# Two attention heads side by side on TensorE, values by channel, and the block export ahead of the slabs

## The reference, cut to what matters

```
q = rms_norm(q) * 64**-0.5 ; k = rms_norm(k)
p = softmax over keys of (q k^T + bias by distance, by three dilated windows)
out = p v
```

## Time and profile before

| | |
|---|---|
| median of 3 runs | 1527.39 us |
| lowest, highest | 1512.98, 1580.74 us |
| the profiled execution | 1512.7 us, span 1510.8 us |
| PE busy | 1414.2 us (94%) |
| DVE, ACT, POOL busy | 504.5, 253.1, 175.2 us |
| mean granted clock | 0.94 |

### The profile page before, as it was taken

One profiled execution on the slowest core, in us unless ns is written; L12 is line 12 of the kernel. 1 busy time (PEld: TensorE's weight loads), 2 busy tenths in 40 slices (PEclk: granted clock), 3 DMA queues, 4 the chain that ended last, 5 costly groups with the idle time before them and its releaser, 6 DMA issues.

```text
span 1510.8 us, 15332 instructions
## 1 busy us (share of the span) xinstructions
PE 1414.2 (94%) x5616; PEld 757.4 (50%) x5616; DVE 504.5 (33%) x1149; ACT 253.1 (17%) x491; POOL 175.2 (12%) x168
## 2 busy tenths in 40 slices
PE   5999989999969999999999859999999999999985
PEld 3444655544437777777455534344444444444432
DVE  2089673233523545555134530211111111111110
ACT  5000223232012323333011100000000000000000
POOL 1000015221000000000000010211110111111111
PEclk9999999999956878899999859999999999999998
DMA  6011010100020101030322139886999999999971
GB/s 258 0 57 56 0 56 1 57 6 22 0 93 5 32 5 32 4 116 1 115 88 94 56 116 424 318 339 243 405 420 403 400 412 397 402 396 398 402 288 22
DMA packets 51273, 262.17 MB, mean 174 GB/s; under 512 B 21571, under 2 KB 21843, under 8 KB 38908
## 3 DMA queue, kind: packets, MB, share of 16 engines
q1 hardware_dynamic: 42684, 244.18, 40.2%
q0 software_dynamic: 8320, 16.81, 4.6%
q10 hardware_dynamic: 192, 0.17, 0.0%
HBM read 247.97 MB, written 23.64 MB: 180 GB/s over the span
## 4 chain that ended last, share of the span: by engine, by line
PE 72%; issue 9%; DMA 6%; DVE 6%; POOL 3%; DVEq 2%; ACT 1%; SPq 0%; POOLq 0%; ACTq 0%
PE ps L1137 19%; PE ps L1139 13%; PE ps L869 9%; PE ps L1046 7%; PE ps L1001 6%; PE ps L1024 4%; PE ps L1013 3%; DMA arena<-in_ex_up 3%; DMA arena<-in_ex_down 2%; POOL arena L1971 2%; PE ps L1123 1%; PE ps L1067 1%; POOL arena L1967 1%; DVEq L1249 1%; DVE arena L1250 1%
## 5 line engine op out<-in xcount | busy, mean ns | idle before, releaser
L1137 PE MATMUL ps<-arena 128*128 128x512 f32 x768 | 338.0, 597 | 1.7 <-ACT arena L1922 0.8
L1137 PEld LDWEIGHTS ps<-arena 128*128 128x128 f32 x768 | 144.7, 192 | 172.5 <-issue 170.1
L1139 PE MATMUL ps<-arena 128*64 128x512 f32 x480 | 212.1, 598 | 7.6 <-DMA arena<-in_ex_up 4.1
L1140 PE MATMUL ps<-arena 128*64 128x512 f32 x480 | 212.2, 598 | 0.0
L873 PE MATMUL ps<-arena 128*128 128x512 f32 x384 | 172.0, 601 | 0.0
L869 PE MATMUL ps<-arena 128*128 128x512 f32 x320 | 137.6, 592 | 0.0
L1139 PEld LDWEIGHTS ps<-arena 128*64 128x64 f32 x480 | 64.4, 138 | 136.5 <-issue 134.5
L1693 DVE TENSOR_TENSOR arena<-arena,ps 128x512 f32<-128x512 f32 x26 | 17.9, 689 | 330.1 <-PE ps L1137 204.1
L873 PEld LDWEIGHTS ps<-arena 128*128 128x128 f32 x384 | 72.5, 194 | 81.7 <-issue 81.6
L1046 PE MATMUL ps<-arena 128*128 128x512 f32 x256 | 111.0, 592 | 0.0
L1001 PE MATMUL ps<-arena 64*128 64x512 f32 (+3 forms) x192 | 96.5, 617 | 14.6 <-DVE arena L1456 13.6
(11 more groups left out here) (296 smaller groups left out, 1298.2 us busy)
## 6 DMA issues: line engine op xcount, KB each, us to landing
arena<-in_ex_gate SPq DMA_DIRECT2D x32, 2048.0 KB, 21.5
arena<-in_ex_up SPq DMA_DIRECT2D x32, 2048.0 KB, 24.3
arena<-in_ex_down SPq DMA_DIRECT2D x32, 2048.0 KB, 24.0
arena<-in_w_in SPq DMA_DIRECT2D x5, 2048.0 KB, 8.0
arena<-in_x SPq DMA_DIRECT2D x16, 512.0 KB, 6.4
arena<-bias_by_distance SPq DMA_DIRECT2D x4, 1024.0 KB, 5.8
arena<-in_w_out SPq DMA_DIRECT2D x8, 512.0 KB, 7.5
out<-arena SPq DMA_DIRECT2D x8, 512.0 KB, 2.7
```

The lines of the kernel that those rows point to most:

```text
L1137: last = mm(ps[:, to, :], rowsT[:, k, :], weights[left][:, k, cols], **f)
L1139: mm(ps[0:HALF, to, :], rowsT[:, k, 0:HALF], weights[left][:, k, cols], **f)
L1140: last = mm(ps[HALF:P, to, :], rowsT[:, k, HALF:P], weights[right][:, k, cols], **f)
```

## The change

Attention steps become 32 double steps: both heads of a pair for one tile. Tiles run from 7 to 0 in pairs 0 and 2, and from 0 to 7 in pairs 1 and 3. Scores are cut in chunks of at most 512 keys; one chunk fills bank 6 with one head and bank 7 with the other, and the reductions run on each head and chunk, with the maxima of two chunks joined after. Values take v as the weight (64 columns) and `probT` as the moving side, head 0 to partitions 0 to 63 of bank 3 and head 1 to 64 to 127, so the result is already channels by tokens. The old turns of `att` (`att_out`) go; instead the reciprocals of the sums are spread over 64 columns each (`rz`), turned (`zt`), copied by ACT to `rzb`, and multiplied onto bank 3 by DVE (`att`). Values of step m-1 stand before the turns of step m, and `probT` has one buffer. The DeltaNet pieces go to two slots of a double step. The first double step's scores stand among the last v tiles. On SP the export of the inverse goes before all but slab 0, slab 0 waits for the k projections alone, and the order constants are loaded at the stage's end. Pool clears the pads in two parts. Seven blocks of constants that nothing reads (`C_LVL`, 896 columns) are dropped, and some buffers move (`slab`, `prob`, `T`, `mixT_dn`, `hg`, `h2s`, `xs`, two of `w_out`, `actT`).

```diff
+STEP_PAIRS = AT_HEADS // 2
+N_STEPS = STEP_PAIRS * TILES
+
+
+def attention_step(m):
+
+    pair, k = divmod(m, TILES)
+    return pair, (k if pair % 2 else TILES - 1 - k)
+
+
+def score_chunks(m):
+
+    wide = (attention_step(m)[1] + 1) * P
+    return [(c0, min(512, wide - c0)) for c0 in range(0, wide, 512)]
+
+
+CHUNKS = [(m, c) for m in range(N_STEPS) for c in range(len(score_chunks(m)))]
+CHUNKS_PER_PAIR = len(CHUNKS) // STEP_PAIRS
...
     attention = []
-    for n in range(n_att + 8):
-        if n < n_att:
-            attention.append((("scores", n), 1.5 * attention_step(n)[1] + 2))
-        if 1 <= n <= n_att:
-            attention.append((("turn", n - 1), 1.5 * attention_step(n - 1)[1] + 2))
-        if 2 <= n <= n_att + 1:
-            attention.append((("values", n - 2), 0.5 * attention_step(n - 2)[1] + 1))
-        if n % 8 == 4 and n >= 12:
-            attention.append((("att_out", n // 8 - 1), 1))
+    for m in range(N_STEPS + 1):
+        if m + 1 < N_STEPS:
+            attention.append((("scores", m + 1, 0), 0.45))
+        if m:
+            attention.append((("values", m - 1), 0.3 * (attention_step(m - 1)[1] + 1) + 0.5))
+            if m % 4 == 0:
+                attention.append((("att", m // 4 - 1), 0))
+        attention.append(("slot", 0))
+        if m < N_STEPS:
+            attention.append((("turn", m), 0.3 * (attention_step(m)[1] + 1) + 0.5))
+            if m % 4 == 3:
+                attention.append((("rz", m // 4), 0))
+        if m + 1 < N_STEPS and len(score_chunks(m + 1)) > 1:
+            attention.append((("scores", m + 1, 1), 0.45))
+        if m < N_STEPS and m % 4 == 3:
+            attention.append((("zt", m // 4), 0.5))
+        attention.append(("slot", 0))
...
+    first = [("scores", 0, c) for c in range(len(score_chunks(0)))]
+    out = []
+    for t in range(TILES):
+        out.append(("v", t))
+        if t >= TILES - 1 - len(first) and first:
+            out.append(first.pop(0))
+    out += first
+    total, done = 0.97 * sum(c for _, c in attention), 0
...
+        if event == "slot":
+            while pieces and pieces[0][1] * total <= done:
+                out.append(pieces.pop(0)[0])
+        else:
+            out.append(event)
...
+        TAKER = ["v" if (n % 2 and TURNS[n][0] == "p") else "a" for n in range(len(TURNS))]
...
+            sp.wait_ge(proj_done, group_end[4])
+            sp.wait_ge(bias_out, 16)
             load_slab(0)
-            load_slab(1)
-            sp.dma_start(moe_c, a["order"]).then_inc(order_in, 16)
             sp.wait_ge(inverse_done, 1)
             sp.dma_start(tb_dram.rearrange("n r c -> n (r c)"), blockT).then_inc(inverse_out, 16)
             sp.dma_start(ttb_dram.rearrange("n r c -> n (r c)"), blockTt).then_inc(inverse_out, 16)
             sp.wait_ge(dn_zero, 1)
             sp.wait_ge(inverse_out, 32)
-            for t in (0, 1, 2, 3):
-                load_T(t)
+            load_T(0)
+            sp.wait_ge(dn_zero, 2)
+            load_T(1)
+            load_slab(1)
+            load_T(2)
+            load_T(3)
             load_slab(2)
...
-                    n = ev[1]
-                    pair, i, hh = attention_step(n)
-                    if n == 0:
+                    m, c = ev[1], ev[2]
+                    pair, i = attention_step(m)
+                    if m == 0:
                         pe.wait_ge(qk_out, 16)
-                        pe.wait_ge(act_took, len(STEPS) - 4)
                         pe.wait_ge(chunk_v, 2 * TILES)
-                    rows = slice(HD * hh, HD * hh + HD)
-                    pe.wait_ge(s_max, n)
-                    for c0 in range(0, (i + 1) * P, 512):
-                        w = min(512, (i + 1) * P - c0)
-                        last = mm(ps[:, 6 + c0 // 512, 0:w], qkT[rows, 0, pair, i * P:(i + 1) * P],
+                    pe.wait_ge(s_max, chunks_before(m, c))
+                    c0, w = score_chunks(m)[c]
+                    for hh in range(2):
+                        rows = slice(HD * hh, HD * hh + HD)
+                        last = mm(ps[:, 6 + hh, 0:w], qkT[rows, 0, pair, i * P:(i + 1) * P],
                                   qkT[rows, 1, pair, c0:c0 + w], start=True, stop=True)
                     last.then_inc(s_scores, 1)
...
-                    n = ev[1]
-                    pe.wait_ge(s_exp, n + 1)
-                    for g, cnt in turn_groups(n):
+                    m = ev[1]
+                    wide = attention_step(m)[1] + 1
+                    pe.wait_ge(s_exp, 2 * m + 1)
+                    for g, cnt in turn_groups(m):
                         if idx >= 2:
                             pe.wait_ge(*taken(idx - 2))
                         for c in range(cnt):
-                            last = tr(ps[:, TB + idx % 2, c * P:(c + 1) * P], prob[:, n % 2, (g + c) * P:(g + c + 1) * P], ident)
+                            hh, b = divmod(g + c, wide)
+                            if (hh, b) == (1, 0):
+                                pe.wait_ge(s_exp, 2 * m + 2)
+                            last = tr(ps[:, TB + idx % 2, c * P:(c + 1) * P], prob[m % 2][:, hh, b * P:(b + 1) * P], ident)
                         last.then_inc(s_turn, 1)
                         idx += 1
...
+                    m = ev[1]
+                    pair, i = attention_step(m)
+                    if m == 0:
+                        pe.wait_ge(act_took, len(STEPS) - 4)
+                    elif m % 4 == 0:
+                        pe.wait_ge(s_att, m // 4)
+                    for who in range(first_turn[("p", m)], last_turn[("p", m)] + 1):
                         pe.wait_ge(*taken(who))
                     for b in range(i + 1):
-                        last = mm(ps[:, PV, n % 8 * HD:(n % 8 + 1) * HD], probT[:, n % 2, b * P:(b + 1) * P],
-                                  v_tok[:, b, pair * P + hh * HD:pair * P + (hh + 1) * HD], start=(b == 0), stop=(b == i))
+                        for hh in range(2):
+                            j = hh * (i + 1) + b
+                            last = mm(ps[HD * hh:HD * hh + HD, PV, i % 4 * P:(i % 4 + 1) * P],
+                                      v_tok[:, b, pair * P + hh * HD:pair * P + (hh + 1) * HD],
+                                      probT[:, j * P:(j + 1) * P], start=(b == 0), stop=(b == i))
                     last.then_inc(s_values, 1)
-                elif ev[0] == "att_out":
-                    i = ev[1]
-                    pe.wait_ge(s_att, i + 1)
+                elif ev[0] == "zt":
+                    g = ev[1]
+                    pe.wait_ge(s_rz, g + 1)
                     pe.wait_ge(*taken(idx - 2))
                     for c in range(4):
-                        last = tr(ps[:, TB + idx % 2, c * P:(c + 1) * P], att[:, c * P:(c + 1) * P], ident)
+                        last = tr(ps[:, TB + idx % 2, c * P:(c + 1) * P], rzx[:, c * P:(c + 1) * P], ident)
                     last.then_inc(s_turn, 1)
                     idx += 1
...
+            pe.wait_ge(s_att, N_STEPS // 4)
...
+                    m, c = ev[1], ev[2]
+                    pair, i = attention_step(m)
+                    if c == 0:
+                        v.wait_ge(slab_in[pair % 2], 16 * (pair // 2 + 1))
+                        if m == 0:
+                            v.wait_ge(proj_done, group_end[4])
+                        elif m == 1:
+                            v.wait_ge(proj_done, len(STEPS))
+                        else:
+                            v.wait_ge(s_turn, last_turn[("p", m - 2)] + 1)
+                    v.wait_ge(s_scores, chunks_before(m, c) + 1)
+                    c0, w = score_chunks(m)[c]
+                    last_chunk = c + 1 == len(score_chunks(m))
+                    for hh in range(2):
+                        done = nc.vector.tensor_tensor_reduce(prob[m % 2][:, hh, c0:c0 + w], ps[:, 6 + hh, 0:w],
+                                                              slab[pair % 2][:, hh, 896 - i * P + c0:896 - i * P + c0 + w],
+                                                              1.0, -3e38, ALU.add, ALU.max, mx[:, m % 2, c, hh:hh + 1])
+                    if not last_chunk:
+                        nc.vector.drain().then_inc(s_max, 1)
+                    else:
+                        nc.vector.drain()
+                        if c:
+                            tt(mx[:, m % 2, 0, :], mx[:, m % 2, 0, :], mx[:, m % 2, 1, :], ALU.max)
+                            nc.vector.drain()
+                        ts(nmx[:, m % 2, :], mx[:, m % 2, 0, :], -1.0, None, ALU.mult).then_inc(s_max, 1)
                 elif ev[0] == "dn":
...
+                elif ev[0] == "rz":
+                    g = ev[1]
+                    v.wait_ge(s_exp, 8 * g + 8)
+                    if g:
+                        v.wait_ge(s_turn, first_turn[("z", g - 1)] + 1)
+                    nc.vector.reciprocal(rZ, Z[:, g % 2, :])
+                    nc.vector.drain()
```

(31 more changed lines are left out.)

172 lines of the change are left out of this document (54 added, 118 removed).

## The result

The changed kernel takes 1453.0 us (median of 4 runs, 1448.8 to 1454.7), the kernel before 1527.0 in the same measurement (4 runs, 1513.0 to 1580.7): a ratio of 0.954, 95% interval 0.947 to 0.961. The prediction was 1448, range 1395 to 1500. The profiled execution took 1454.7 us, its span is 1452.9. Medians and ranges here are of all runs; some executions run in a slower state at a lower granted clock, and the ratios leave these out. The two medians are 74.0 us apart, the two profiled executions 58.0: that of the kernel before, 1512.7, was among its fastest. The account that follows is of the profiled executions.

A forecast was written before the change was run, and what follows sets the result against it. PE was taken to set the pace of the 302.0 us mixer stage, with 94 us at half clock. A stage of 224 at full clock plus 12 for the clock, 236, gave 1448 us with the first wait; range 1395 to 1500.

The forecast's parts named there:

- The sum: Whole kernel: 1512.7 less the mixer stage's 302.0 plus 236, with 1 us for the first wait, gives 1448 us.
- Part 1, the start: Mixer stage's start: earlier inverse export, written by 409 to 414, removes the 11.8 us gap; 1 us of wait taken.
- Part 2, side by side: Two heads' scores and values at once on PE cost what one head's did: 49.1 us a pair instead of 65.8.
- rival (c): Mixer stage's values: the change doesn't put them side by side, 31 us more, 1478 us; chance 7%.
- The drain: Values on PE: changing tiling mode drains 0.1 us more at either end in 32 double steps, 6 us above the forecast.
- Part 3, the loop: Mixer stage's loop of waits between PE, DVE and ACT: 10.3 us a step at w = 8, stage 224 at full clock.
- My 13 us for pieces that follow one another: Mixer stage's wide steps: DeltaNet pieces of one tile wait for DVE's answers, 0.8 us in each of 16 steps.
- Part 4, the clock: Mixer stage: one fall to 1.2 GHz taken, at narrow steps, about 12 us, bounds 0 and 47; stage 236.
- signs of being wrong: Mixer stage profile: values' halves starting one after the other, clock at 0.50 after 420, or DVE busy above 85%.
- (a): Mixer stage: everything overlaps, idle goes, no overflow of pieces and no clock fall; stage 193, kernel 1404 us; chance 12%.
- (b): Mixer stage: 94 us at half clock remain, wherever they fall; stage 271, kernel 1482 us; chance 13%.
- (d): Mixer stage: gaps in every step's loop keep the clock at 1.2 GHz for the whole stage, 1591 us; chance 4%.

The follow-up runs named there:

- e1: Changed kernel with SP's old order back (inverse exported after all projections and both slab loads) and first scores behind the v tiles: 1466.1 us, ratio 0.960.
- b1: Kernel before, with SP writing the two inverse exports ahead of the wait for all projections and the slab loads: 1504.9 us, ratio 0.996.
- e3: Changed kernel with the values' two loops exchanged, all blocks of head 0 before those of head 1: 1467.8 us, ratio 0.962 to the kernel before.
- e4: Changed kernel with PE waiting for head 0's scores before issuing head 1's in each chunk: 1528.7 us, ratio 1.003 to the kernel before.
- e5: Changed kernel with tiles running from 0 to 7 in every pair: 1455.7 us, ratio 0.957 to the kernel before.
- e7: Changed kernel with all DeltaNet pieces after the attention and SP's T loads behind the slabs: 1505.5 us (one run).
- e10: Changed kernel with the turns of the reciprocals (zt) moved behind the second slot of DeltaNet pieces: 1449.5 us, ratio 0.949 to the kernel before.
- e8: Changed kernel with ACT copying two of three groups of turns to probT instead of one of two: 1449.8 us, ratio 0.949 to the kernel before.
- e12: Changed kernel with both zt behind the second slot of pieces and ACT taking two of three copies of turns: 1450.2 us, ratio 0.950.
- e9: Changed kernel with SP's old start order, first scores behind the v tiles, and tiles from 0 to 7 in every pair: 1467.9 us, ratio 0.961.
- e6: Changed kernel with the values of step m-1 ahead of the first scores of step m+1 instead of behind them: 1473.3 us, ratio 0.968.

## Why the prediction was right, point by point

- **The sum.** 1448 against 1453.0; stage 236 against 238.0. In the terms that I used: PE's work at full clock 188 predicted, 181.7 measured; idle beside it 36 (224 less 188) and 38.1; the clock 12 and 18.2. Two errors of 6 us, in the work and in the clock, cancel, which is luck; 2 of the 6 of work are two score groups that stand among the v tiles, ahead of the stage, where I had counted them inside. The profiled execution took 1454.7, 7 above the forecast: 2 are the stage's, 5 lie outside it, where I took 1 and found 6. The forecast was for an execution like the profiled one, so its error is these 7.
- **Part 1, the start: right.** Inverse written by 409.7 (409 to 414 predicted), no idle of PE where I took 1 us. DVE still waited for it, 3.62 us instead of none, off the path. The first chunk's reductions began behind it at 410.35; the joined maximum of the step came at 416.97, 2 us past the "before 415" that I gave, since the second chunk's scores lie behind another v tile (414.16). V tile 7 hid it all the same. e1 prices the part at 13 us, the gap alone. My reading that this gap brought the 49.3 us of low clock has a limit: in the new loop a gap of 12.4 brought 7.9 after it, and in the old one half the gap brought nearly as much as the whole (b1, 47.7 against 48.9).
- **Part 2, side by side: right, the largest part, and larger than its term.** Scores of 512 keys 1.05 us (1.05), values of 8 blocks 1.90 (1.8). e3 prices the values at 15 us of the kernel, where rival (c) had 31 of PE's work: eight blocks in turn take 1.36 us more than side by side (3.26 and 1.90), 0.17 a block and not 0.215, and the stage had 21.7 us more of them busy, not 31. For the scores side by side I had 34 us (18.5 to 10.1 in each of four pairs). e4 gives back 62 in the stage, of which, by the estimate above, some 15 are the wait's own and some 31 the clock's. That the same edit brings long low stretches back was in none of my terms.
- **The drain.** Both heads' values take 0.19 us above 32 x 0.0535 (half of my 0.107 a pair), where one head's took 0.11 above their streaming before: 0.08 us more in each of 32 double steps, 2.6 us. The Trainium skill, page "TensorEngine Tiling (Array Packing)", section "Key Properties", says that a change of tiling mode drains TensorE, and I had 6 us by it if both ends counted; the trace agrees in the direction, with 2.6 us, under half of the size.
- **Part 3, the loop: right in kind, near in size partly by luck.** The first step of w = 8 takes 9.75 us (10.3), but with 2.4 us of pieces in it where I had 4.1. DVE has 142.5 of 238.0 us, 60% (69%; the terms that I named come to 149 us, not to the 155 that I wrote). PE's idle rises by 21.3, released by DVE at the scores (7.2), the turns (10.3 and 2.5) and `zt` (8.3). I had named the first; the turns wait more, since DVE's copy stands behind two reductions. My 13 us for pieces that follow one another aren't seen as such: pieces wait 3.3 us in two places (L959, 2.6 the longest), and the rest is the waits above.
- **Part 4, the clock: the mis-sized term.** I expected one fall or two at the narrow steps, for 12 us. It fell eight times, at narrow and at wide steps, for 3.4 or 6.8 us each, and cost 18.2; falls after 420 were among my own signs of being wrong. Right was that no long low stretch would stay, for a reason that I had only half: I had the shorter gaps, and left out the scores side by side (e4), without which the long ones come back. The order down and up, on which I had put it, does nothing that e5 could show.
- **The rivals.** (a) fell with the idle; (b) had the falls come back "wherever they fall", which is what they do, at 37.5 us of 94; (c) was tested by e3; (d) didn't come. The Trainium skill, page "TensorE: Matmul & The Clock Gate", section "A second HAM failure mode: psum-queue depth-cycling", describes small idles between groups of matmuls that make the clock swing between its two levels. The windows here show such a swing, 1.00 to 0.50 and back eight times in 238 us with PE idle in pieces of 0.2 to 3.0; its price was 8% of the stage, and the kernel was faster all the same. That the idles cause it isn't shown: e7's attention has as much idle in less time and fell twice.

Open: why each of the eight falls is where it is. e10, e8 and e12 had three to six, at other places, with nearly the same idle. Nor is it shown whether the scores' use of the array acts on the clock by itself or through the work that it saves: e4 changes both, and adds a wait to every chunk. Each length of a low stretch is of one execution, and b1's second shows how much that can differ.

## What to carry to other kernels

Where a matmul contracts over 64 rows, look for a second one that can use the other 64 at the same time, with a bank of its own; the same for results of 64 partitions. Read what that is worth from a pair of the same form in the trace, and count the loop anew afterwards, since the work that covered the other engines' answers has halved too: here PE gained 57 us in work, lost 21 of them to idle, and got 28 more from the clock. Of a gap at the start of a stage, find every transfer that ends near it before pricing one of them: with the export alone moved, the slab took its place.

## What the runs showed that I had not expected

- How long the clock stays at 1.2 GHz after a fall went with how the scores use the array, though not without exception. With one head's 64 rows at a time it stayed 48.9 us after PE's return, 47.7 in b1, and for up to 27.3 and 20.5 in the loop (kernel before, e4), but also for 3.4 only (b1's second fall, three in e4); with two heads' 128 rows at once 7.9 and 9.2 us after an idle of 12.4 and 12.3 (e1, e9), and at most 10.2 in the running loop (e6, e10; 6.8 in the changed kernel). In e7's pieces, with no scores beside them, it stayed for up to 20.5.
- Alternating weights every 128 columns between the two halves of the array costs nothing that shows: 0.059 us an instruction with the drain, against 0.10 in turn. The issue order alone (e3) decides it.
